# Four SBUF buffers of the matmul inputs moved by 48 and 40 bytes within their 64-byte lines

## What is computed

```
h = layer_norm(ALPHA * h + mixer(h));  h = layer_norm(ALPHA * h + (silu(g) * u) @ w_down)   # g, u = split(h @ w_gu)
x = x + mixed @ w_out;                 u = relu(rmsnorm(x) @ w_ff1);  x = x + (u * u) @ w_ff2
```

## Time and profile before

| | |
|---|---|
| median of 3 runs | 1364.02 us |
| lowest, highest | 1363.88, 1364.83 us |
| span of the profiled execution | 1362.7 us |
| TensorE busy | 1335.2 us, 11455 matmuls |
| VectorE busy | 933.0 us |
| ScalarE busy | 675.1 us |
| read from memory | 224.40 MB, 165 GB/s over the span |

### The profile page before, as it was taken

How to read it: one execution, slowest core, us unless ns; L and a number is a source line. 1 busy time by engine, 2 the same in 40 slices (tenths; PEclk the granted TensorE clock), 3 DMA queues, 4 the chain that set the end, 5 groups by cost and what they waited for, 6 DMA issues and landing times.

```text
span 1362.7 us, 27289 instructions
## 1 busy us (share of the span) xinstructions
PE 1335.2 (98%) x11455; PEld 1299.2 (95%) x11455; DVE 933.0 (68%) x1249; ACT 675.1 (50%) x838; POOL 58.8 (4%) x31
## 2 busy tenths in 40 slices
PE   5899999999999999999999999999999999999999
PEld 4599999999999999999989999999999999999998
DVE  8966976547865986556896687774457867877542
ACT  5774643334765643344656544444345644544332
POOL 6910000000000000000000000000000000000000
PEclk9999999999999999999999999999999999999999
DMA  8676576665443586666454545566664535556662
GB/s 155 156 186 185 135 208 185 185 186 184 146 136 106 142 216 185 184 186 179 132 155 125 185 155 192 182 183 186 186 186 124 155 124 186 186 186 183 189 182 63
DMA packets 342814, 227.90 MB, mean 167 GB/s; under 512 B 22616, under 2 KB 337792, under 8 KB 342592
## 3 DMA queue, kind: packets, MB, share of 16 engines
q1 hardware_dynamic: 341200, 226.33, 57.8%
q10 hardware_dynamic: 1520, 0.20, 0.1%
HBM read 224.40 MB, written 1.05 MB: 165 GB/s over the span
## 4 chain that ended last, share of the span: by engine, by line
PE 88%; DVE 5%; ACT 4%; issue 1%; POOL 1%; SPq 0%; DMA 0%; DVEq 0%; ACTq 0%; POOLq 0%
PE PS L414 27%; PE PS L415 27%; PE PS L416 27%; DVE w_lo L395 2%; ACT w_hi L390 1%; PE PS L1313 1%; DVE xn L1107 1%; DMA c_rows<-in_ssm_c_re_dram 0%; PE PS L1715 0%; DVE xn L1102 0%; PE PS L2382 0%; PE PS L1297 0%; DVE sqr L1069 0%; PE PS L2393 0%; PE PS L1325 0%
## 5 line engine op out<-in xcount | busy, mean ns | idle before, releaser
L395 DVE TENSOR_TENSOR w_lo<-raw,w_hi 128x2048 fp32r<-128x2048 f32 x207 | 473.4, 2290 | 158.4 <-ACT w_hi L390 157.4
L414 PE MATMUL PS<-x_hi,w_hi 128*128 128x256 f32 x1792 | 511.7, 286 | 0.5 <-DVE w_lo L395 0.4
L415 PE MATMUL PS<-x_lo,w_hi 128*128 128x256 f32 x1792 | 506.9, 283 | 0.0
L416 PE MATMUL PS<-x_hi,w_lo 128*128 128x256 f32 x1792 | 506.8, 283 | 0.0
L390 ACT ACTIVATE w_hi<-raw 128x2048 fp32r<-128x2048 f32 x207 | 395.1, 1909 | 215.1 <-PE PS L416 213.7
L414 PE MATMUL PS<-hid_hi,w_hi 128*128 128x256 f32 x1248 | 354.7, 284 | 0.0
L415 PE MATMUL PS<-hid_lo,w_hi 128*128 128x256 f32 x1248 | 353.1, 283 | 0.0
L416 PE MATMUL PS<-hid_hi,w_lo 128*128 128x256 f32 x1248 | 353.1, 283 | 0.0
L414 PEld LDWEIGHTS PS<-x_hi,w_hi 128*128 128x128 f32 x1792 | 343.3, 192 | 5.2 <-issue 2.6
L415 PEld LDWEIGHTS PS<-x_lo,w_hi 128*128 128x128 f32 x1792 | 343.5, 192 | 0.1
L416 PEld LDWEIGHTS PS<-x_hi,w_lo 128*128 128x128 f32 x1792 | 343.4, 192 | 0.0
(11 more groups left out here) (388 smaller groups left out, 1322.1 us busy)
## 6 DMA issues: line engine op xcount, KB each, us to landing
raw<-in_w_ff_dram SPq DMA_DIRECT2D x128, 512.0 KB, 4.6
raw<-in_ffn_w_gu_dram SPq DMA_DIRECT2D x88, 512.0 KB, 5.1
raw<-in_w_in_dram SPq DMA_DIRECT2D x68, 512.0 KB, 4.7
raw<-in_sb_w_qkv_dram SPq DMA_DIRECT2D x24, 512.0 KB, 4.5
raw<-in_ffn_w_down_dram SPq DMA_DIRECT2D x20, 512.0 KB, 5.2
raw<-in_ssm_w_glu_dram SPq DMA_DIRECT2D x16, 512.0 KB, 5.7
raw<-in_w_out_dram SPq DMA_DIRECT2D x16, 512.0 KB, 4.6
raw<-in_ssm_w_out_dram SPq DMA_DIRECT2D x8, 512.0 KB, 4.5
```

The costliest lines, as they stand in the source:

```text
L395: nc.vector.tensor_tensor(w_lo[s][:, :], raw[s][:, :], w_hi[s][:, :].bitcast(F32), ALU.subtract).then_inc(lo_done, 1)
L414: nc.tensor.matmul(dst, lhs_hi, r_hi, start=start, stop=False, skip_group_check=True)
L415: nc.tensor.matmul(dst, lhs_hi, r_lo, start=False, stop=False, skip_group_check=True)
L416: return nc.tensor.matmul(dst, lhs_lo, r_hi, start=False, stop=stop, skip_group_check=True)
```

## The change

The regions xh, xl, hh and hl grow by 64 bytes. x_hi and x_lo then begin 12 elements (48 bytes), hid_hi and hid_lo 10 elements (40 bytes) behind the start of their region. Five pairs or single tensors that share hh and hl move by 64 bytes. Everything laid out behind moves by 64 to 256 bytes. No instruction is added, removed or moved in its order.

```diff
-                           ("wh", 4 * CH * RING), ("wl", 4 * CH * RING), ("res", 8192), ("xh", 8192), ("xl", 8192),
-                           ("hh", 32768), ("hl", 32768), ("xc", 8192), ("sq", 4096), ("sg", 6144), ("zt", 2048),
+                           ("wh", 4 * CH * RING), ("wl", 4 * CH * RING), ("res", 8192), ("xh", 8192 + 64), ("xl", 8192 + 64),
+                           ("hh", 32768 + 64), ("hl", 32768 + 64), ("xc", 8192), ("sq", 4096), ("sg", 6144), ("zt", 2048),
...
-        x_hi = sb("x_hi", [P, KT, T], "xh", 0, F32R)
-        x_lo = sb("x_lo", [P, KT, T], "xl", 0, F32R)
-        hid_hi = sb("hid_hi", [P, 32, T], "hh", 0, F32R)
-        hid_lo = sb("hid_lo", [P, 32, T], "hl", 0, F32R)
+        def shifted(name, region, by, rows, n):
+
+            whole = sb(name, [P, rows * n + 16], region, 0, F32R)
+            return whole[:, by:by + rows * n].rearrange("p (k n) -> p k n", n=n)
+
+        x_hi, x_lo = shifted("x_hi", "xh", 12, KT, T), shifted("x_lo", "xl", 12, KT, T)
+        hid_hi, hid_lo = shifted("hid_hi", "hh", 10, 32, T), shifted("hid_lo", "hl", 10, 32, T)
...
-        raw_hi = sb("raw_hi", [P, KT, T + 2], "hh", 22 * 4 * T, F32R)
-        raw_lo = sb("raw_lo", [P, KT, T + 2], "hl", 22 * 4 * T, F32R)
+        raw_hi = sb("raw_hi", [P, KT, T + 2], "hh", 22 * 4 * T + 64, F32R)
+        raw_lo = sb("raw_lo", [P, KT, T + 2], "hl", 22 * 4 * T + 64, F32R)
...
-        qkv = sb("qkv", [P, 16, T], "hh", 16 * 4 * T)
-        v_tok = sb("v_tok", [P, 2, D], "hl", 24 * 4 * T)
+        qkv = sb("qkv", [P, 16, T], "hh", 16 * 4 * T + 64)
+        v_tok = sb("v_tok", [P, 2, D], "hl", 24 * 4 * T + 64)
...
-        ztile = sb("ztile", [P, 10, T], "hl", 16 * 4 * T)
-        sig_g = sb("sig_g", [P, 16, T], "hh", 16 * 4 * T)
+        ztile = sb("ztile", [P, 10, T], "hl", 16 * 4 * T + 64)
+        sig_g = sb("sig_g", [P, 16, T], "hh", 16 * 4 * T + 64)
```

## The result

| | before | after |
|---|---|---|
| median | 1363.95 us (4 runs, 1363.82 to 1364.83) | 1355.19 us (4 runs, 1354.78 to 1357.44) |
| span of the profiled execution | 1362.7 us | 1353.2 us |
| ratio of the times | | 0.9936, 95% interval 0.9924 to 0.9949 |

What follows compares the result with a forecast made beforehand. TensorE's start-to-start matmul distance was taken as the bound. x's -15.9 and hid's -6.4 us, times 0.92, gave -20.5 us: span 1342.2 from 1362.7, median 1343.5 us, with an 8-in-10 range of 1310 to 1369.

Steps and rivals of the forecast that it cites:

- the distance of the starts: Whole kernel: time is number of matmuls times start-to-start distance, about 120 ns, where 256 columns need 106.7 ns.
- the start address counts: Moving operand's start offset changes matmul distance: 120.9 ns at offset 0 against 118.0 at 48.
- Price for x: Matmuls moving x, now at 48 bytes: -2.9 ns each over 5472, -15.9 us.
- Price for hid: Matmuls moving hid, now at 40 bytes: -1.7 ns each over 3744, -6.4 us.
- the 22.3: Forecast gain in us from faster x and hid matmuls, before the 0.92 share reaching the end.
- Sorted by offset over all eight passes: Matmuls moving raw_hi/raw_lo, six per offset in eight passes of 48; mean distances 118.0 to 120.9 ns, used as prices.
- the likeliest error: Gain's size named as most likely error: six matmuls in a row don't tell where hundreds settle.
- moves by 64 and so keeps its place in a 64-byte line: Buffers sharing the enlarged regions, and everything behind them, were said to keep their place in a 64-byte line.
- x as weights, 0: Token-major v chunks, 384 matmuls with x stationary: taken as 0, bounds 1.1 us either way.
- What reaches the end, 92%: Layer-norm transitions, 8% of time, are paced by VectorE; so 0.92 of the gain arrives, -20.5 us.
- The rival that it settles at 120 again: Steady x and hid streams return to 120 ns despite the offsets, no gain: 1364 us, chance 0.13.
- The rival that crossing lines of 16 bytes costs: hid at 40 touches 65 pieces, not 64: +1.9 ns, +7.0 us; slower if x gains under 1.3 ns; 1371 us, chance 0.13.

Runs made afterwards that it cites:

- h1: Against the kernel before: x at 16 and hid at 40 bytes, high and low parts at the same place modulo 256; 1353.79 us.
- e2: Against the changed kernel: x back at offset 0, hid kept at 40 bytes, enlarged regions kept; 1360.69 us.
- e4: Against the changed kernel: x and hid all back at offset 0, enlarged regions kept; 1361.60 us.
- f1: Against the kernel before: xh, xl, hh enlarged by 128 bytes, hl by 64, no offsets, so low parts lie 128 off the high ones modulo 256; 1346.81 us.
- e3: Against the changed kernel: hid at 48 bytes instead of 40, so x and hid are both at 48; 1348.70 us.
- i1: Against the kernel before: x and hid both at 32 bytes, high and low parts at the same place modulo 256; 1340.09 us.
- g1: Against the kernel before: x and hid both at 48 bytes, high and low parts at the same place modulo 256, weights unmoved; 1351.74 us.
- f3: Against the kernel before: both weight parts 48 bytes further, x and hid at offset 0 but moved by 128 through the pad; 1349.82 us.
- f4: Against the kernel before: weights, x and hid all given a 48-byte offset, with the pad putting x at 176 modulo 256; 1359.02 us.
- f2: Against the kernel before: x and hid at 48 bytes, with low parts 128 bytes off the high ones modulo 256; 1342.69 us.
- e1: Against the changed kernel: hid back at offset 0, x kept at 48 bytes; 1354.68 us.

## Why the forecast was right in kind and wrong in size

- **That the distance of the starts bounds the kernel** and that nothing else would move: right. Instruction counts, the other engines' times and the waits are the same.
- **That the start address counts**: right. The Trainium skill (SBUF — State Buffer, Who interferes with whom) says that TensorE never waits on anyone. No run here shows a wait for another engine, so it isn't contradicted; but mean distances from 116.7 to 121.0 ns for one and the same instruction in eighteen kernels show that no such rule makes the distance independent of addresses.
- **Price for x, -2.9 ns and -15.9 us**: measured -1.96 ns a matmul and -10.9 us, and 1.7 of it given back in pauses, so -9.2. In the settled stages it is 117.8 ns. Mis-sized by a third.
- **Price for hid, -1.7 ns and -6.4 us**: this is the step that failed. Measured +0.2 ns and +0.6 us; of the 12 us by which x and hid together missed the 22.3, 7 are hid's. Three kernels show what stands in its place: at 40 bytes with the parts alike the stream gives 0.7 ns (h1), and where the change puts the parts, 168 and 232 modulo 256, it gives nothing (after, and e2 with 119.92).
- **Both come from one step**: "Sorted by offset over all eight passes" took a mean over six matmuls at an offset as the price of that offset. But each distance depends on what went before (at offset 0 the single ones go from 113 to 125 ns), the passes never settle, and the settled value isn't their mean. The forecast named this as the likeliest error and still put its point on the mean.
- **"moves by 64 and so keeps its place in a 64-byte line"** looked modulo 64 alone. The high and low parts came apart by 64 modulo 256, and e4 (64 apart) and f1 (128 apart) show that such a distance counts by itself: -3 us and -18 us without any offset.
- **x as weights, 0**: -0.7 us, inside its bounds of 1.1 us either way.
- **What reaches the end, 92%**: of x's 10.9 us, 9.2 came through, 85%. Right in kind: the chain that ended last now lies for 85% on TensorE and 11% on VectorE, where it was 88% and 5%.
- **The rival that it settles at 120 again** is what happened to hid, 120.14 ns, in an uneven pattern with the same sum. The rivals were posed for x and hid together; asked for each buffer they would have given the measured case, x with its gain and hid without: 1362.7 - 15.9 x 0.92 = 1348 of span, nearer to 1353.2.
- **The rival that crossing lines of 16 bytes costs**: at 120/64 = 1.9 ns for a line, e3's hid (48) and after's hid (40) differ by one line in 65, 1.9 ns, and 1.9 is what lies between 120.14 and 118.24. But this rival also wants 16, 32 and 48 to be as 0, and h1, i1 and g1 have 118.1, 116.7 to 116.9 and 118.3 against 119.9. It doesn't order the offsets. Its slower side wanted x to gain less than 1.3 ns, and x gained 1.96. The two reasons that the prediction gave against it from the raw passes were none: a raw row of 1032 bytes touches 65 pieces of 16 bytes at every one of the eight offsets, so these passes say nothing of lines.

What stays open: the mechanism. The places of both operands count, of the moving one (g1, with the weights unmoved) and of the stationary one (the token chunks). Whether only their relative places count, and with what period, wasn't settled, since the pads of f3 and f4 moved x and hid by 128 with the weights. Nor is it known what picks one of two patterns.

## What to carry to other kernels

When float32r matmuls of 256 columns follow each other without a pause, look at the distance between starts, not at busy time, and try the start addresses of moving and stationary tiles: it costs no instruction and was worth 1.8% here. Take the price from a stream that stays at one set of addresses for hundreds of matmuls, in every stage, and not from a mean over a mixed one. Moving one buffer moves all behind it: write down the place of every operand modulo 256 ahead of and behind such a change.

## What the runs showed of the hardware that was not expected

- The same places modulo 256 mostly give the same mean distance in either buffer and in other kernels: (0, 128) 117.78 and 117.70 ns, (48, 48) 118.34 and 118.33, (32, 32) 116.76, 116.89 and 116.74, (48, 112) 117.94, 117.94 and 117.92 in three kernels. Where more than one pattern occurs it holds less well: (168, 232) 120.14 and 119.92, (128, 192) 120.15 and 120.32.
- Settled streams have exact sums for a triple of matmuls: 360.0 ns at the start, 353.3 in x of the changed kernel, 355.0 at (48, 48), 350.0 at (32, 32) and 346.7 in some stages of f2, of x and of hid. Single distances in them go from 112 ns (f1) to 131 (e1).
- For some addresses two or three such values exist (e4: 120.0 and 117.8 ns for x; e1: 117.8, 120.0 and 121.1 for hid). A stage mostly keeps one for hundreds of matmuls, but e2's hid stream changed at 920.9 us, without a pause.
- ScalarE's and VectorE's work doesn't depend on the offsets tried: VectorE is busy for 932.0 to 933.3 us in all eighteen kernels, ScalarE for 674.8 to 676.6.
